# Mixture-of-experts results added in place: a scatter with addition into one row per token, the routing weight applied as each expert's result leaves PSUM

## The reference, cut to what matters

```
D_MODEL = 1024; SEQ = 512; DEC_BATCH = DEC_SEQ = 8; MOE_EXPERTS = 16; MOE_TOP_K = 2; MOE_HIDDEN = 512
# hier_moe: x are the 576 normed rows
g_prob, g_idx = top_k(softmax(x @ w_rg + b_rg), 1)          # one group of four
e_top, e_idx  = top_k(logits of that group's experts, 2)    # two experts in it
weights = softmax(e_top) * g_prob
combine[n, expert] = weights                                # zero for the 14 others
hg = x @ w_gate[e]; hu = x @ w_up[e]
act = silu(hg) * hu * combine[:, e]
y = sum over e of act @ w_down[e]
# decoder_layer, then the last norm
x = x + gate2(c) * y
y_out = adaLN_RMSNorm(x; c_final)
```

## Time and profile before

| | us |
|---|---|
| median of 3 runs | 1371.2 (1370.54 to 1372.87) |
| profiled execution, its own time | 1375.12 |
| its span | 1373.3 |

### The profile page before, as it was taken

The page is one execution under the profiler, slowest core; times in us unless marked ns, Lnnn a source line. Parts: engine busy times, 40 slices in busy tenths (PEclk is TensorE's granted clock), DMA queues, the critical chain, the costliest instruction groups (busy, mean ns, idle before and its releaser), DMA issues. The chain is left out here.

```text
span 1373.3 us, 17850 instructions
## 1 busy us (share of the span) xinstructions
PE 1226.6 (89%) x7111; PEld 935.8 (68%) x7111; DVE 671.4 (49%) x900; ACT 543.2 (40%) x872; POOL 206.0 (15%) x237
## 2 busy tenths in 40 slices
PE   3799999999999999998789999999997999999920
PEld 0477877777778878886656667667676887777710
DVE  0615522322161213113666451336876888888746
ACT  2333214102282134116333332212555777777621
POOL 2401300010000010002200021000261222222210
PEclk8699999999999999998799999999999999999965
DMA  9412212244434452547789995521759999999831
GB/s 363 162 62 85 101 38 72 82 164 183 159 127 126 165 194 88 175 171 292 261 303 360 350 319 208 164 100 41 275 185 332 376 370 377 368 375 373 286 146 69
DMA packets 125193, 289.95 MB, mean 211 GB/s; under 512 B 10084, under 2 KB 10204, under 8 KB 120456
## 3 DMA queue, kind: packets, MB, share of 16 engines
q1 hardware_dynamic: 106280, 236.49, 48.5%
q0 software_dynamic: 18848, 52.53, 10.9%
HBM read 270.37 MB, written 26.18 MB: 216 GB/s over the span
## 5 line engine op out<-in xcount | busy, mean ns | idle before, releaser
L965 PE MATMUL psum<-part,part 128*128 128x512 f32 (+1 forms) x1088 | 444.3, 408 | 9.9 <-DVE part L2306 9.7
L966 PE MATMUL psum<-part,part 128*128 128x512 f32 (+1 forms) x1088 | 429.7, 395 | 0.0
L967 PE MATMUL psum<-part,part 128*128 128x512 f32 (+1 forms) x1088 | 429.6, 395 | 0.0
L965 PEld LDWEIGHTS psum<-part,part 128*128 128x128 f32 (+1 forms) x1088 | 227.9, 209 | 73.6 <-issue 23.2
L967 PEld LDWEIGHTS psum<-part,part 128*128 128x128 f32 (+1 forms) x1088 | 227.5, 209 | 40.3
L966 PEld LDWEIGHTS psum<-part,part 128*128 128x128 f32 (+1 forms) x1088 | 228.5, 210 | 36.4 <-issue 0.5
L2275 DVE TENSOR_TENSOR part<-arena,part 128x2048 fp32r<-128x2048 f32 x96 | 218.8, 2290 | 50.6 <-ACT part L1716 49.5
L1820 DVE TENSOR_TENSOR part<-arena,part 128x2048 fp32r<-128x2048 f32 x42 | 96.4, 2300 | 244.8 <-PE psum L1007 220.3
L1716 ACT ACTIVATE part<-arena 128x2048 fp32r<-128x2048 f32 x94 | 179.8, 1920 | 66.9 <-DMA arena<-in_w_up_dram 29.3
L1491 ACT ACTIVATE arena<-psum 128x512 f32<-128x512 f32 (+4 forms) x142 | 77.2, 570 | 253.4 <-PE psum L967 200.6
L953 PE MATMUL psum<-cst,arena 128*128 128x128 f32 (+3 forms) x857 | 124.1, 286 | 46.3 <-DMA cst<-in_consts_dram 12.4
(11 more groups left out here) (271 smaller groups left out, 1087.7 us busy)
## 6 DMA issues: line engine op xcount, KB each, us to landing
arena<-in_w_in_dram SPq DMA_DIRECT2D x34, 1024.0 KB, 5.2
arena<-in_cache_kv_w_dram SPq DMA_DIRECT2D x16, 2048.0 KB, 11.7
arena<-in_w_gate_dram SPq DMA_DIRECT2D x32, 1024.0 KB, 9.9
arena<-in_w_up_dram SPq DMA_DIRECT2D x32, 1024.0 KB, 10.0
arena<-in_w_down_dram SPq DMA_DIRECT2D x32, 1024.0 KB, 10.0
arena<-in_w_ada_dram SPq DMA_DIRECT2D x24, 1024.0 KB, 7.1
arena<-in_cache_kv_w_dram SPq DMA_DIRECT2D x16, 1024.0 KB, 9.0
arena<-in_w_ada_final_dram SPq DMA_DIRECT2D x8, 1024.0 KB, 8.0
```

Of the source, the lines that this page charges most:

```text
L965: nc.tensor.matmul(out_, hi, w_hi, start=start, stop=False)
L966: nc.tensor.matmul(out_, hi, w_lo, start=False, stop=False)
L967: last_product[0] = nc.tensor.matmul(out_, lo, w_hi, start=False, stop=stop)
```

## The change

- `yd` has one row a token. It is set to zero early: POOL fills the tile `zeros` and writes it to `yd` with five DMAs, between its additions for the first norm and those for the gating's norm. DVE waits for them before it writes the low parts that share that memory.
- `scatter` adds its rows to `yd` (`compute_op=ALU.add`).
- The second number of a slot is the token's routing weight in place of a destination row. The two weights are made before the slot writes start, and written into `token_places`' copy; `result` multiplies by the weight of each row as it leaves PSUM. So ACT's `result` now waits for the slots of its expert (`dest_in`).
- The slots for `result` and `scatter` are loaded right behind the scatter of the expert before (`load_places`); those of expert 0 behind `load_modulation(1)` and the wait for the slot writes.
- At the end `yd` is loaded with one row a token, five DMAs without a wait between them, and ACT's and DVE's two weighting operations a tile are gone.
- For the last expert `gated` and `hidden_high`/`hidden_low` go ahead of the split of the second down half; `gated` also goes ahead of that of the first.

```diff
--- before.py
+++ after.py
@@ -103,13 +103,13 @@
-    return np.stack([0 * row + TOK, 0 * row + 2 * TOK], axis=1).astype(np.uint32)
+    return np.stack([0 * row + TOK, 0 * row], axis=1).astype(np.uint32)
...
-    a = np.stack([np.stack([tok, 2 * tok + k], axis=-1) for k in range(2)], axis=1)
+    a = np.stack([np.stack([tok, 0 * tok], axis=-1) for k in range(2)], axis=1)
...
@@ -340,9 +340,11 @@
         tok_u = stat[:, 600:620].bitcast(U32).rearrange("p (k i a) -> p k i a", k=2, i=TILES)
+        tok_w = stat[:, 600:620].rearrange("p (k i a) -> p k i a", k=2, i=TILES)[:, :, :, 1]
         row_u = stat[:, 570:580].bitcast(U32).rearrange("p (k i) -> p k i", k=2)
         slot_u = stat[:, 580:584].bitcast(U32).rearrange("p (b n) -> p b n", b=2)
         dest_u = stat[:, 584:588].bitcast(U32).rearrange("p (b n) -> p b n", b=2)
+        dest_w = stat[:, 584:588].rearrange("p (b n) -> p b n", b=2)[:, :, 1:2]
...
@@ -373,8 +375,9 @@
-        yg = at(4 * SLOT, TILES, 2, D)
-        junk_end = at(4 * SLOT + TILES * 2 * D, D)
+        yg = at(4 * SLOT, TILES, D)
+        junk_end = at(4 * SLOT + TILES * D, D)
+        zeros = at(KEPT0 + D, D)
...
@@ -506,7 +509,7 @@
-        yd = dram("yd", (2 * TOK + CAP, D))
+        yd = dram("yd", (TOK + CAP, D))
...
@@ -786,6 +789,10 @@
             for i in range(TILES):
                 add_shift(i, x0[:, i, :], mod[:, 0, i // 4, :], hn_scaled, hn_done)
+            nc.gpsimd.memset(zeros, 0.0).then_inc(y_zero, 1)
+            pool.wait_ge(y_zero, 1)
+            for i in range(TILES):
+                pool.dma_start(yd[i * P:i * P + ROWS[i], :], zeros[0:ROWS[i], :]).then_inc(y_zeroed, 16)
             for i in range(TILES):
                 add_shift(i, mix[:, i, :], lnb, vn_scaled, vn_done)
...
@@ -878,9 +885,11 @@
             for par in range(2):
-                pool.dma_start(yd[2 * TOK + par:2 * TOK + par + 1, :], h2d[par:par + 1, :]).then_inc(y_out[par], 16)
+                pool.dma_start(yd[TOK + par:TOK + par + 1, :], h2d[par:par + 1, :]).then_inc(y_out[par], 16)
             load_modulation(1)
             pool.wait_ge(tok_out, 16 * 2 * TILES)
+            pool.dma_start(dest_u[:, 0, :], slots_d[0:CAP, :]).then_inc(dest_in[0], 16)
+            pool.wait_ge(y_zeroed, 16 * TILES)
             rounds = rounds_of(pool)
...
@@ -897,39 +906,37 @@
-
+            def load_places(pair_, par):
+
+                row = ((pair_ % PAIRS) * 2 + par) * EROWS + (pair_ // PAIRS) * CAP
                 pool.dma_start(dest_u[:, par, :], slots_d[bass.ds(row, CAP), :]).then_inc(dest_in[par], 16)
+
+            def scatter(after, par):
+
                 pool.wait_ge(dest_in[par], after * 16)
                 pool.wait_ge(y0_out, after * 2 + par)
                 pool.wait_ge(y1_out, after * 2 + par)
 
                 pool.wait_ge(y_out[1 - par], after * 16 if par == 0 else after * 16 + 16)
                 waited()
-                pool.indirect_dma_start(yd, bass.IndirectOffsetOnAxis(ap=dest_u[:, par, 1:2], axis=0),
-                                        yb[:, par, :], None, bounds_check=2 * TOK - 1, oob_is_err=False
-                                        ).then_inc(y_out[par], 16)
+                pool.indirect_dma_start(yd, bass.IndirectOffsetOnAxis(ap=dest_u[:, par, 0:1], axis=0),
+                                        yb[:, par, :], None, bounds_check=TOK - 1, oob_is_err=False,
+                                        compute_op=ALU.add).then_inc(y_out[par], 16)
 
             with pool.Fori(0, rounds * PAIRS - 1) as it:
                 for par in range(2):
                     fetch(it + 1 + par, 1 - par, it * 4 + 2 * par + 4, it + 1)
-                    scatter(((it % PAIRS) * 2 + par) * EROWS + (it // PAIRS) * CAP, it + 1, par)
-            for par in range(2):
-                scatter((E_ALL - 2 + par) * EROWS + (rounds - 1) * CAP, rounds * PAIRS, par)
+                    scatter(it + 1, par)
+                    load_places(it + par, 1 - par)
+            scatter(rounds * PAIRS, 0)
+            load_places(rounds * PAIRS - 1, 1)
+            scatter(rounds * PAIRS, 1)
             pool.wait_ge(xg_in[0], rounds * (PAIRS * 16) + 16)
             for par in range(2):
                 pool.wait_ge(y_out[par], rounds * (PAIRS * 16) + 16)
             waited()
-            def load_outputs(i):
-
-                n = ROWS[i]
-                pool.dma_start(yg[0:n, i, :, :], yd[2 * i * P:2 * (i * P + n), :].rearrange("(p k) n -> p k n", k=2)
-                               ).then_inc(yg_in[i % 2], 16)
-
             for i in range(TILES):
-                if i >= 2:
-                    pool.wait_ge(yg_in[i % 2], 16 * (i // 2))
-                load_outputs(i)
+                pool.dma_start(yg[0:ROWS[i], i, :], yd[i * P:i * P + ROWS[i], :]).then_inc(yg_in[i], 16)
...
@@ -1730,9 +1737,11 @@
             def result(par, done, after):
                 act.wait_ge(y_out[par], after * 16)
+                act.wait_ge(dest_in[par], after * 16)
                 for c, (filled, out_) in enumerate(((y0_filled, y0_out), (y1_filled, y1_out))):
                     act.wait_ge(filled, done + 1)
-                    nc.scalar.activation(yb[:, par, c * CH:(c + 1) * CH], psum[:, 5 + c, :], ACT.Copy).then_inc(out_, 1)
+                    nc.scalar.activation(yb[:, par, c * CH:(c + 1) * CH], psum[:, 5 + c, :], ACT.Copy,
+                                         scale=dest_w[:, par, :]).then_inc(out_, 1)
...
@@ -1778,24 +1787,17 @@
             last = rounds * E_ALL
             high(4, last * 16)
+            hidden_high(last)
             high(5, last * 16)
-            hidden_high(last)
             result(1, last, rounds * PAIRS)
-            for i in range(TILES + 1):
-                if i < TILES:
-                    n = ROWS[i]
-                    act.wait_ge(yg_in[i % 2], 16 * (i // 2 + 1))
-                    nc.scalar.activation(yg[0:n, i, 0, :], yg[0:n, i, 0, :], ACT.Copy,
-                                         scale=w1[0:n, i:i + 1]).then_inc(y1_scaled, 1)
+            for i in range(TILES):
+                n = ROWS[i]
+                act.wait_ge(x2_done, i + 1)
                 if i:
-                    n = ROWS[i - 1]
-                    act.wait_ge(x2_done, i)
-                    if i > 1:
-                        act.wait_ge(sq3, i - 1)
-                    nc.scalar.activation(junk_end[0:n, :], x1[0:n, i - 1, :], ACT.Square,
-                                         accum_out=ss[0:n, i - 1:i]).then_inc(sq3, 1)
-                    act.wait_ge(var3, i)
-                    nc.scalar.activation(rs[0:n, i - 1:i], rs[0:n, i - 1:i], ACT.Sqrt).then_inc(sqrt3, 1)
+                    act.wait_ge(sq3, i)
+                nc.scalar.activation(junk_end[0:n, :], x1[0:n, i, :], ACT.Square, accum_out=ss[0:n, i:i + 1]).then_inc(sq3, 1)
+                act.wait_ge(var3, i + 1)
+                nc.scalar.activation(rs[0:n, i:i + 1], rs[0:n, i:i + 1], ACT.Sqrt).then_inc(sqrt3, 1)
...
@@ -1926,6 +1928,7 @@
             split_to(S0["gb"][2])
+            dve.wait_ge(y_zeroed, 16 * TILES)
             for i in range(4):
                 turn_tile_lo("ob", i, obT, obT_lo)
...
@@ -2291,37 +2294,38 @@
-            V.tensor_copy(row_u, rowf).then_inc(rows_done, 1)
-            slots_of(2)
-            low(1, 8)
-            rounds = rounds_of(dve)
...
             dve.wait_ge(rt_exp, 2)
             own(V.tensor_reduce(gp, eg, AX.X, ALU.add))
             own(V.reciprocal(gp, gp))
             own(V.tensor_scalar(w1, w2, 1.0, None, ALU.add))
             own(V.reciprocal(w1, w1))
             own(V.tensor_tensor(w1, w1, gp, ALU.mult))
-            own(V.tensor_tensor(w2, w2, w1, ALU.mult))
+            own(V.tensor_copy(tok_w[:, 0, :], w1))
+            own(V.tensor_tensor(tok_w[:, 1, :], w2, w1, ALU.mult))
+            V.tensor_copy(row_u, rowf).then_inc(rows_done, 1)
+            slots_of(2)
+            low(1, 8)
+            rounds = rounds_of(dve)
+
...
@@ -2341,30 +2345,28 @@
             last = rounds * E_ALL
+            gated(last)
             low(4, last * 6 + 5)
-            gated(last)
+            hidden_low(last)
             low(5, last * 6 + 6)
-            hidden_low(last)
...
             def add_experts(i):
                 n, s = ROWS[i], i // 4
-                y1, y2 = yg[0:n, i, 0, :], yg[0:n, i, 1, :]
-                x = x1[0:n, i, :]
-                dve.wait_ge(y1_scaled, i + 1)
-                own(V.scalar_tensor_tensor(out=y1, in0=y2, scalar=w2[0:n, i:i + 1], in1=y1, op0=ALU.mult, op1=ALU.add))
-                own(V.tensor_tensor(y1, y1, mod[0:n, 2, s, :], ALU.mult))
-                V.tensor_tensor(x, x, y1, ALU.add).then_inc(x2_done, 1)
+                y, x = yg[0:n, i, :], x1[0:n, i, :]
+                dve.wait_ge(yg_in[i], 16)
+                own(V.tensor_tensor(y, y, mod[0:n, 2, s, :], ALU.mult))
+                V.tensor_tensor(x, x, y, ALU.add).then_inc(x2_done, 1)
                 dve.wait_ge(x2_done, i + 1)
```

(12 more changed lines are left out.)

13 lines of the change are left out of this document (6 added, 7 removed).

## The result

| | before | after |
|---|---|---|
| median, us | 1370.9 (1370.51 to 1372.87) | 1389.4 (1387.74 to 1392.26) |
| ratio, 95% interval | | 1.0132 [1.0118, 1.0147] |
| profiled execution, us | 1375.12 | 1387.74 |
| its span, us | 1373.3 | 1386.1 |

The change makes the kernel 1.3% slower, 18.5 us by the medians. The forecast was 1374.3. The sign was the forecast's, the size was not: 1389.4 lies beyond the forecast's own range of 1370 to 1380 and at the very end of the whole range, 1389.

What follows compares the result with a forecast made beforehand. It took PE and the DMA engines to be both at their limit in the loop. Terms +8.1 +6.6 -4.0 +1.5 -9.1 = +3.1 us on 1371.2 gave 1374.3; range 1363 to 1389, likeliest 1370 to 1380.

Steps and rivals of the forecast that it cites:

- What bounds the kernel: In the loop: PE and the DMA engines both at their limit, so added DMA work per expert is paid.
- The zeros, the weights made earlier: Before the loop: zero writes and eight short DVE operations cost nothing, covered by idle time of POOL and DVE.
- The first places: Start of the loop: expert 0's `result` waits for places loaded behind the modulation, +8.1 us.
- Rival C: Start of the loop: expert 0's places land in time, taking away the 8.1; 1366.2 us, chance 0.09.
- rival E: Start of the loop: half of the wait is hidden, +4 instead of +8.1; 1370.2 us, chance 0.08.
- The scatters in the loop: Loop: adding doubles the scatter's 0.80 us an expert, 9.6 over twelve, less 3 of cushion: +6.6 us.
- Rival B: Loop and last scatter: adding is free for the DMA engines; 1365.2 us, chance 0.26.
- Rival D: Loop: adding takes three times a plain scatter, places may come late; 1384.7 us, interval over 19.5, chance 0.20.
- the 3 us of cushion: Loop start: after the wait expert 3's gate loads land sooner, giving 3 us the loop uses up before it pays.
- The last expert: End of the loop: reordered splits let PE's down product start 3.4 us earlier, 5.1 at full rate; taken as -4.0.
- The last scatter: After the loop: adding makes the unshared 3.23 us scatter longer, bounds 3.2 and 6.5; +1.5 us.
- The end: After the last scatter: shorter first load -1.3, no ACT scaling -1.2, five DVE operations gone -6.6; -9.1 us.

Runs made afterwards that it cites:

- E9: E1 with each plain scatter issued a second time, to a spare array, `result` waiting for both; 1388.9 us, ratio to before 1.0124.
- E1: The change with a plain scatter in place of the adding one; 1368.7 us, ratio to before 0.9984.
- E5: The kernel before with `load_modulation(1)` issued between the last two scatters instead of ahead of the loop; 1364.9 us, ratio 0.9950.
- E7: The change with `load_modulation(1)` issued behind the loop; 1376.8 us, ratio to before 1.0034.
- E2: The kernel before with an adding scatter, `yd` keeping two rows a token and zeroed early; 1395.7 us, ratio 1.0182.
- E4: The kernel before with only the last expert's order changed on ACT and DVE; 1367.7 us, ratio 0.9981.
- E3: The change with expert 0's places loaded ahead of the modulation's loads; 1383.8 us, ratio to before 1.0089.
- E8: E7 with plain scatters to two rows a token, second rows of tiles 1 to 4 added by loads at the end; 1366.2 us, ratio to before 0.9958.

## Why the prediction was right and wrong

**What bounds the kernel** was read rightly: two engines at their limit, and "whatever DMA work the change adds to an expert, the loop pays". E9 shows just that.

**The zeros, the weights made earlier**: at nothing, and E1 has both in it and is not slower than before. In the traces PE turns the third tokens, behind both, at 1027.42 for 1027.45 before (1028.41 in E1). Not tested apart.

**The first places**: +8.1 foreseen, +8.3 measured; `result` at 1043.50 for "near 1044", tokens at 1064.13 for 1063 to 1065. Rival C falls with it, rival E too. PE stood 15.84 us and then worked at 0.50 of its clock from 1050 to 1054, as foreseen. The reading came from two rows of the trace before, a load that was not in the path then but had the same place in the same queue. What wasn't seen is that most of the wait can be had back, in either kernel, by moving the modulation's loads (E5, E7).

**The scatters in the loop** is the step that failed: +6.6 foreseen, +14.5 measured. The mechanism, the doubling, was right, and its sign with it: E9 and the packets show it. Rival B (nothing extra) falls. Rival D falls as a mechanism, since an adding packet takes twice a plain one and not three times, and since ACT never again waits for its places after the first; but by the numbers D, with 1384.7 and an interval over 19.5, was nearer than the forecast. That the range came within half a microsecond of the result is owed to D's wrong mechanism, and so is luck. The term was mis-sized in two places. First, 0.80 an expert was said where it is 1.24 (E7 against before) to 1.42 (E2 against before), and 1.34 for the change against E1. It had been half of the queue's 8.6%, and only that queue was counted. In E9 the second scatter's own packets took about that, 0.89, and the interval still rose by 1.28: the weights' packets became longer beside them. In the change the software queue took 1.04 more per expert than before and 1.13 more than E1. Second, the 3 us of cushion. Only the first interval, 18.02, ran at PE's pace. What the late start and the new order of loads can give back is seen in E1 against before: 18.30 for 18.44, 1.7 us in twelve. And before, with three intervals at 18.0, had a cushion of its own, of which the change has one left. So 12 x 1.34 less 1.7 is 14.4, where 12 x 0.80 less 3 was said.

**The last expert**: -4.0 foreseen, -3.5 measured, in the change and alone (E4). The -4.0 was taken between 3.4, the earlier start of the down product, and 5.1, with PE at full rate. No run shows the 4.0: the product starts 3.6 us sooner after the last tokens and lasts as long as before, 7.31 us for 7.18, since the half clock came again. Busy time by stretch after:

```profile
1324.00:1328.00 4.00, 0.88 (x6) 0.62 (x6) 3.52 (x4) 2.40 (x2) 0.00 (x0) 1.00 0.12 22
1328.00:1332.00 4.00, 4.00 (x12) 3.08 (x12) 3.97 (x3) 0.00 (x0) 0.00 (x0) 0.59 0.02 4
```

PE did 0.88 us of work in 4 and was then at 0.59 of its clock for the next 4, as in the earlier trace rows.

**The last scatter**: +1.5 foreseen, +2.7 measured (5.95 for 3.23; plain in E1 3.22). The bound of "all of it doubled", 6.5, was the nearer; that most of the 3.2 us was way and not bytes was wrong, or the way is doubled as well.

**The end**: -9.1 foreseen. Load -1.1 for -1.3, scaling -1.2, DVE -7.0 for -6.6, together -9.3; tiles at 5.23 for 5.2. Nothing else came late there.

In the account of the profiled executions the miss is 9.7 us (12.8 less 3.1): 7.9 in the loop, 1.2 at the last scatter, the rest 0.6. By the medians it is 15.1, since the two profiled executions stand on opposite sides of their medians. What makes executions of one kernel differ by several us was not found: E1's lie between 1364.05 and 1372.37, E9's between 1388.16 and 1389.44. So E9 is 20.2 over E1 by the medians and 16.7 by the profiled runs.

## What to carry to other kernels

Where the DMA engines' share is at 1 in a loop, count an accumulating DMA as two plain ones of the same rows (E9), price it by what it does to the interval and not by its own queue's share, and ask whether the sum can be made where the engines are idle. In a queue that is served in order, look at what stands ahead of each small load that someone waits for; moving the large load away gave 0.5% with no other change, but in front of another small load it made a new wait of up to 2.9 us (the gap of 4.5 for 1.6), whose worth in time the runs did not resolve. A cushion that one sees in some intervals before is already part of the mean, and a change that lengthens the others can lose it.

## What the runs showed that was not expected

An adding scatter also costs POOL more to issue: 1.59 to 1.84 us for L922 in the change against 0.99 to 1.23 for the plain one in E1, while in E9 two plain ones took up to 1.23 and 1.00. Single ones are dearer, 3.57 in E3 (above) and up to 3.62 in E2, and up to 2.24 plain in the kernel before; what made them so was not found. It hid behind POOL's idle time here. The adding scatter that landed last took 5.95, 6.21, 6.03 and 7.17 us in the change, E2, E3 and E7, the last of them with the modulation's loads in the queue ahead of it; plain ones took 3.22 in E1, 3.36 in E9 and, with those loads ahead, 3.25 in E5 and 3.85 in E8.
